# The last layer's expert results gated as they leave PSUM, and a final merge with all gathers issued at once

## The reference, cut to what matters

```python
hdn = jax.nn.silu(xb @ w1[e]) * (xb @ w3[e])      # per block of tokens of one expert
ys  = hdn @ w2[e]
y   = ys[dest] * flat_w[order][:, None]           # two rows a token, weighted
out = jax.ops.segment_sum(y, tok, num_segments=N)
xl  = xl + gt2 * out                              # gt2: one row of 1024, from the modulation vectors
return rmsnorm(xl, final_g)                       # after the last layer
```

## Time and profile before

| | us |
|---|---|
| median of 3 runs | 2804.71 (2804.48 to 2804.72) |
| the profiled execution's own time | 2803.35 |
| its span | 2801.6 |
| PE busy | 2571.0 (92% of the span) |
| DVE busy | 1082.8 (39%) |
| ACT busy | 865.5 (31%) |
| POOL busy | 478.1 (17%) |
| first weight chunk of layer 0's experts asked for | 984.9 |
| the same of layer 1 | 2173.9 |
| end of its last matmul | 2735.8 |

### The profile page before, as it was taken

How to read it: one execution, slowest core, us unless ns; L and a number is a source line. 1 busy time by engine, 2 the same in 40 slices (tenths; PEclk the granted TensorE clock), 3 DMA queues, 4 the chain that set the end, 5 groups by cost and what they waited for, 6 DMA issues and landing times. The chain is left out here.

```text
span 2801.6 us, 68712 instructions
## 1 busy us (share of the span) xinstructions
PE 2571.0 (92%) x28274; PEld 1803.8 (64%) x28275; DVE 1082.8 (39%) x2462; ACT 865.5 (31%) x1881; POOL 478.1 (17%) x590
## 2 busy tenths in 40 slices
PE   7999999999989849999999599999998699999990
PEld 6888788878745537777777484455444477777770
DVE  3134333433454532222222366556665322222225
ACT  3222322323210003333333355334500133333333
POOL 0111111121121012222222210000020122222223
PEclk9999999999999969999999799999999799999995
DMA  6322223132345287999999740000232999999995
GB/s 260 120 97 100 95 104 134 61 126 74 140 152 200 75 355 305 416 416 395 416 416 416 268 144 30 31 30 30 115 150 105 389 403 416 417 416 416 416 368 183
DMA packets 128670, 644.72 MB, mean 230 GB/s; under 512 B 18865, under 2 KB 31441, under 8 KB 72609
## 3 DMA queue, kind: packets, MB, share of 16 engines
q1 hardware_dynamic: 94912, 540.05, 48.5%
q0 software_dynamic: 17984, 57.16, 5.7%
q10 hardware_dynamic: 15648, 45.71, 4.2%
HBM read 578.29 MB, written 64.57 MB: 229 GB/s over the span
## 5 line engine op out<-in xcount | busy, mean ns | idle before, releaser
L1668 PE MATMUL PS<-wt,xT 128*32 128x256 f32 x13056 | 752.9, 381 | 38.3 <-DVE xT L1797 25.3
L1668 PEld LDWEIGHTS PS<-wt,xT 128*32 128x32 f32 x13056 | 513.0, 111 | 238.7 <-issue 47.9
L1613 ACT ACTIVATE y<-PS 32x256 f32<-32x256 f32 x816 | 306.3, 375 | 304.2 <-PE PS L1683 297.0
L1683 PE MATMUL PS<-wt,hidT 128*32 128x256 f32 x6528 | 395.2, 379 | 3.5 <-ACT y L1613 3.5
L1797 DVE STREAM_TRANSPOSE xT<-xg 128x256 f32<-128x256 f32 x206 | 91.8, 446 | 664.2 <-PE PS L1668 655.0
L1683 PEld LDWEIGHTS PS<-wt,hidT 128*32 128x32 f32 x6528 | 256.8, 110 | 99.3 <-issue 4.4
L720 PE MATMUL PS<-hT,slab 128*128 128x256 f32 x1280 | 296.2, 386 | 6.3 <-DVE low L613 3.5
L720 PEld LDWEIGHTS PS<-hT,slab 128*128 128x128 f32 x1280 | 239.9, 192 | 42.9 <-issue 6.5
L433 POOL TENSOR_SCALAR prob<-prob,inv 128x640 f32<-128x640 f32 (+2 forms) x80 | 130.3, 1629 | 662.2 <-DVE inv L628 662.2
L1573 POOL DMA_INDIRECT xg<-h_d,ib x212 | 208.3, 983 | 166.8 <-POOL ib L1570 166.0
L511 ACT ACTIVATE prob<-prob,low 128x640 f32<-128x640 f32 (+2 forms) x160 | 117.6, 735 | 300.2 <-DVE low L613 300.2
(11 more groups left out here) (247 smaller groups left out, 2653.4 us busy)
## 6 DMA issues: line engine op xcount, KB each, us to landing
wt<-in_w SPq DMA_DIRECT2D x256, 1024.0 KB, 11.9
wt<-in_w2s SPq DMA_DIRECT2D x128, 1024.0 KB
aw<-in_ada_w SPq DMA_DIRECT2D x48, 1024.0 KB, 4.9
ys_d<-y ACTq DMA_DIRECT2D x204, 128.0 KB
slab<-in_slabs SPq DMA_DIRECT2D x24, 512.0 KB, 3.3
tab<-in_tables SPq DMA_DIRECT2D x8, 1408.0 KB, 7.5
ys_d<-zero POOLq DMA_DIRECT2D x4, 2560.0 KB, 9.6
x_d<-x_p ACTq DMA_DIRECT2D x18, 512.0 KB, 4.8
```

The lines of the kernel that those rows point to most:

```text
L1613: ins = a.activation(y[rows, q * QD:q * QD + QD], PS[STRIP * q:STRIP * q + STRIP, DOWN, 0:QD], ACT.Copy)
L1668: mm = t.matmul(PS[32 * g:32 * g + 32, UP, 0:QD], xT[:, k * 32:k * 32 + 32], wt[b][:, q, c * 1024 + g * QD:c * 1024 + g * QD + QD], start= ...
L1683: mm = t.matmul(PS[32 * g:32 * g + 32, DOWN, 0:QD], hT_[:, k * 32:k * 32 + 32], wt[b][:, q, c * 1024 + g * QD:c * 1024 + g * QD + QD], sta ...
```

## The change

Five things are changed together.

- **Store in layer 1.** VectorE gets a new step in each turn of its loop, `gated`, behind `hidden`: it multiplies the whole PSUM tile (128x256) of the item before by a gate tile and writes it to a quarter of the columns of `y`. ScalarE no longer copies; its queue stores 128 partitions of 1 KB to the same 32 rows of `ys_d`. The first call, ahead of any result, only raises `y_ok`, and a last one behind the loop takes the last item.
- **Gate tile.** Four loads behind the first 12 weight chunks of layer 1 fill it (`early_loads`), and VectorE waits for them in `before_items_vector`.
- **Gathers.** All 16 are issued one after the other, each tile into its own buffers; nothing waits between them.
- **Merge.** As the rows are gated already, tiles 0, 2, 4, 6 and 7 take two VectorE operations for the sum, and tiles 1, 3 and 5 are summed by TensorE in PSUM, by products with the identity and with two diagonal matrices of the weights. ScalarE takes the squares and roots as before, VectorE the last product. Stores go straight from the tiles' buffers.
- **Recurrent vectors in layer 0.** The series moves behind the first transpose, into `behind_first_rows_vector`.

The core of the diff:

```diff
@@ class MergeMid
+            def behind_first_rows_vector(self, v):
+                r, n_ = self.lru, [7]
...
+                v.wait_ge(self.once, 7)
                 v.wait_ge(self.exp_ok, 1)
                 once(v.tensor_scalar(s2, z_, 2.0, None, ALU.add))
                 once(v.reciprocal(s2, s2))
...
@@ class MergeEnd
+            ON_PE = (1, 3, 5)
...
+                self.y = [(late1 if n < 6 else late2)(f"y_c1{n}", [P, 2, D]) for n in range(NTL)]
+                self.gate = flat(RLs[:, :, :])[:, 0:QD]
...
             def early_loads(self, sp):
-                pass
+                for q in range(4):
+                    at_q = mod_d[0, (NMOD + 5) * D + q * QD:]
+                    sp.dma_start(self.gate[32 * q:32 * q + 32, :], bass.AP(tensor=at_q.tensor, offset=at_q.offset, ap=[[0, 32], [1, QD]])
+                                 ).then_inc(self.gate_in, 16)
...
             def before_items_vector(self, v):
-                pass
+                v.wait_ge(self.gate_in, 64)
...
             def stores(self, sp):
                 for n in range(NTL):
                     sp.wait_ge(self.ob_ok, n + 1)
-                    sp.dma_start(out[0, n * P:(n + 1) * P, :], self.ob[n % 2][:, :]).then_inc(self.x_out[n % 2], 16)
...
+                    sp.dma_start(out[0, n * P:(n + 1) * P, :], self.y[n][:, 1, :]).then_inc(self.x_out, 16)
+                sp.wait_ge(self.x_out, 16 * NTL)
 
             def gather(self, g):
                 g.wait_ge(self.ys_ok, 1)
                 for n in range(NTL):
-                    if n >= 2:
-                        g.wait_ge(self.m_ok, n - 1)
-                    for k, yk in enumerate((self.y0, self.y1)):
-                        g.indirect_dma_start(out=yk[n % 2][:, :], out_offset=None, in_=ys_d[:, :],
+                    for k in range(2):
+                        g.indirect_dma_start(out=self.y[n][:, k, :], out_offset=None, in_=ys_d[:, :],
...
+            def tensor(self, t):
+                t.wait_ge(self.x_in, 16 * NTL)
+                for i, n in enumerate(self.ON_PE):
+                    t.wait_ge(self.dg_ok, 2 * i + 2)
+                    t.wait_ge(self.y_in[n], 32)
+                    for h in range(2):
+                        half = slice(h * 512, (h + 1) * 512)
+                        t.matmul(PS[:, 2 * i + h, :], ident[:, :], self.xa[:, n, half], start=True, stop=False)
+                        for k in range(2):
+                            mm = t.matmul(PS[:, 2 * i + h, :], self.diag[n][k][:, :], self.y[n][:, k, half], start=False, stop=(k == 1))
+                    mm.then_inc(self.pe_ok, 1)
...
                 def add(n):
...
+                    v.scalar_tensor_tensor(out=x, in0=x, scalar=tabs[1][:, 0, n:n + 1], in1=self.xa[:, n, :],
+                                           op0=ALU.mult, op1=ALU.add).then_inc(self.row_ok, 1)
+                    v.wait_ge(self.row_ok, 2 * m + 1)
+                    v.scalar_tensor_tensor(out=x, in0=self.y[n][:, 1, :], scalar=tabs[1][:, 1, n:n + 1], in1=x,
+                                           op0=ALU.mult, op1=ALU.add).then_inc(self.row_ok, 1)
...
                 add(0)
                 for n in range(NTL):
-                    if n + 1 < NTL:
+                    if n + 1 < NTL and n + 1 not in self.ON_PE:
                         add(n + 1)
                     norm(n)
@@ def experts
+            y_part = lambda j: y[:, j * QD:(j + 1) * QD]
...
+                    def store_gated(n, j):
+
+                        a.wait_ge(y_ok, n + 2)
+                        a.dma_start(ys_d[bass.ds(n * STRIP, STRIP), :].rearrange("t (q c) -> q t c", q=4), y_part(j)
+                                    ).then_inc(y_out[j], 16)
...
+                            if l:
+                                store_gated(n, j)
+                            else:
+                                store(n, i, j)
...
+                    def gated(n, i, j):
+
+                        v.wait_ge(used[5], n + 1)
+                        v.wait_ge(y_out[(j - 1) % DEEP], 16 * i + 16)
+                        v.tensor_tensor(y_part((j - 1) % DEEP), PS[:, DOWN, 0:QD], merge.gate, ALU.mult).then_inc(y_ok, 1)
+
                     rows_T(0, 0, 0)
+                    merge.behind_first_rows_vector(v)
                     with v.Fori(0, count) as i:
...
                             hidden(n)
+                            if l:
+                                gated(n, i, j)
+                    if l:
+                        gated(count * DEEP, count, 0)
```

More of the change, by code:

```diff
@@ L1357, in begin @@
                 nm = lambda x: sem(f"{x}_c1")
[L1358 to L1362, removed]
+                self.gate_in, self.fin_in, self.x_in, self.x_out = nm("gate"), nm("fin"), nm("x_in"), nm("x_out")
+                self.y_in = [gather_sem(f"y_in{n}_c1") for n in range(NTL)]
+                self.dg_ok, self.pe_ok, self.row_ok, self.sum_ok, self.sqrt_ok, self.rs_ok, self.ob_ok = (
+                    nm(x) for x in ("diag", "on_pe", "rows_made", "sum", "sqrt", "rs", "ob"))
             def early_loads(self, sp):
-                pass
+                for q in range(4):
+                    at_q = mod_d[0, (NMOD + 5) * D + q * QD:]
+                    sp.dma_start(self.gate[32 * q:32 * q + 32, :], bass.AP(tensor=at_q.tensor, offset=at_q.offset, ap=[[0, 32], [1, QD]])
+                                 ).then_inc(self.gate_in, 16)
             def early_scalar(self, a):
@@ L1427, in scalar @@
[L1427 to L1432 removed]
+                for n in self.ON_PE:
+                    for k in range(2):
+                        a.activation(self.diag[n][k][:, :], ident[:, :], ACT.Identity, scale=tabs[1][:, k, n:n + 1]).then_inc(self.dg_ok, 1)
+                a.activation(self.rt[:, NTL:NTL + 1], epst[:, :], ACT.Sqrt)
@@ L1596, in _ @@
                     count = a.value_load(npi[0:1, 0:1], **most)
-                    a.sem_inc(y_ok, 1)
+                    if not l:
+                        a.sem_inc(y_ok, 1)
                     for j in range(DEEP):
-                        a.sem_inc(y_out[j], 16)
+                        a.sem_inc(y_out[j], 32 if l and j == DEEP - 1 else 16)
                     def tanh(n):
@@ L1622, in _ @@
                             tanh(n + 1)
-                            store(n, i, j)
+                            if l:
+                                store_gated(n, j)
+                            else:
+                                store(n, i, j)
                     for j in range(DEEP):
-                        a.wait_ge(y_out[j], 16 * count + 16)
+                        a.wait_ge(y_out[j], 16 * count + (32 if l and j == DEEP - 1 else 16))
                     a.sem_inc(ys_ok, 1)
```

82 lines of the change are left out of this document (35 added, 47 removed).

## The result

The changed kernel takes 2921.71 us (median of 4 runs, 2920.53 to 2924.3), the kernel before 2804.72 beside it (2804.48 to 2806.67): the ratio is 1.042 (95% interval 1.0408 to 1.0433). I had forecast 2882 and a range to 2918; the direction held, and the time is 3.7 us outside the range.

The account below looks back on a forecast made before the run. TensorE, busy 92% of the span, was taken to bound the kernel. Terms -5.4 + 100.3 - 0.2 - 17.1 = +77.6 us on the 2801.6 us span gave 2879.2, a forecast time of 2882.3 us, range 2840 to 2918.

Parts of the forecast that it names:

- Four engines: Layer 1's gated store, outer dimension 4: runs on four DMA engines, the same each time, 1.29 us more an item each.
- The loop: Layer 1's item loop: the four engines' added store load makes the last weights late, +100.3 us.
- What would show it: Signs in the profile after: TensorE waits for weights, items of 6.2 us, mean DMA share about 0.85, twelve engines idle.
- Start of layer 1: Gate loads queued behind twelve weight chunks delay the first transpose 2 to 6 us, covered while weights set the pace: 0.
- Start of layer 0: The series for the decay rates moves behind the first transpose, which then starts earlier: -5.4 us.
- To the first gather: From the last down product to the first final gather: shorter until the store's issue, longer store, together -0.2 us.
- The merge: First final gather to the end: transfers set the pace, pairs 3.23 us apart, stores delay the last pair: -17.1 us.
- low-clock price: Final merge: an instruction of TensorE's tiles estimated at 0.9 us at half clock, against 0.45 us at full clock.
- low-clock rival: Final merge: TensorE's low clock sets its pace, -7.8 us instead of -17.1, 2892 us with four engines; chance 0.07.
- the rival of 16 engines: Layer 1's stores use all 16 engines or wander over them, so the kernel gains: 2784.7 us; chance 0.20.

Follow-up runs that it names:

- the last kernel: The changed kernel with the store in four transfers, the gate's loads in front of the weights, and VectorE's merge sums two tiles ahead: 2774.12 us, ratio 0.99.

## Why the prediction was wrong in size, point by point

- **Four engines** (right). The short packets said so before, and 132 packets a store say so after. That they are the same four each time fits as well: the weights are left on four engines' worth of share, and the stores take turns with just those.
- **The loop, +100.3 against +138.7** (this term failed). The step was "four engines get 1.29 us more an item. Every weight chunk is spread over all 16 and is there only when the slowest has finished": I priced the store by the engine time of its pieces and made the weights wait for it. In the changed kernel it is the store that waits for the weights. Its 32 packets an engine take turns with 8 KB packets, 11 us a store in place of 1.63; four buffers and the queue cover some items, then ScalarE stands in the issue and TensorE behind it. The weights catch up, twelve engines run idle and then all weights are through, the stores go at 1.5 us each, and it begins again. 25 of the loop's stores took 4 us or more to issue; 25 items at 10.8 us instead of 5.18 would be 140 us more, an estimate that covers the loss. The mechanism that I had priced exists: the four engines do fall behind, and with 2 KB packets, where the turns are short, it costs 60 us. In the change as made TensorE never waited for it, and what it would cost at 8 KB without the turns was not measured. So the term came as near as it did by luck, for a reason that was not the acting one.
- **What would show it** followed the same error. TensorE waiting for weights: not one such wait, and 26 only with 2 KB packets. A mean share near 0.85: 0.81 from 2210 to 2700, as a mean of stretches near 1.0 and others at 0.2 to 0.3. Twelve engines do idle in the latter, but just there TensorE runs at its old pace, so it is no sign of a wait for DMA. An item at 6.2 us: 6.7.
- **The rule of the Trainium skill** ("DMA: Bandwidth & Descriptors", section "Why a DMA increments its semaphore by 16 and not by 1") was right: an outer 4 gives four engines. I had not weighed another section of that page, "Queues, rings and completion order", by which an engine goes round its queues packet by packet. The trace agrees that turns go by count and not by bytes (beside 8 KB neighbours a store of 1 KB pieces took 10.6 to 11.2 us and one of 512 B pieces 10.3), and it shows one piece of each queue in a turn (78 to 73).
- **Start of layer 1, covered: 0 against +7.0** (wrong). The size was near (2 to 6 us forecast), the cover was not there: I let the weights set the pace behind it, and they never did. 6.6 us came back when the gate was loaded first. It was my own condition "with all 16 engines it is on the path", which in fact held for four as well.
- **Start of layer 0, -5.4 against -3.0.** Right for the part by itself (-6.3, -3.6 to -9.0); this kernel's load landed 2.3 us later.
- **To the first gather, -0.2** (right: -0.1).
- **The merge, -17.1 against -21.6.** The pairs came at the pace I gave them: in the last kernel tile 0's rows are used at 2738.60 and tile 4's at 2750.90, 3.08 us a pair against 3.23. Wrong was that each output store delays the last pair by 1.25 us. The rows were all there, and VectorE ran with gaps of at most 0.15 us from 2901.57 on:

```profile
2901.57 0.16 DVE L1469 RECIPROCAL rs_c<-rt_c 128x1 f32<-128x1 f32 x1 [3.56 <-ACT rt_c L1436]
...
2913.80 1.28 DVE L1460 SCALAR_TENSOR_TENSOR y_c<-y_c,w,xa_c 128x1024 f32<-128x1024 f32 x1
...
2918.14 1.28 DVE L1471 SCALAR_TENSOR_TENSOR y_c<-y_c,rs_c,fin_c 128x1024 f32<-128x1024 f32 x1
```

  Tile 7's first sum starts 31.0 us behind the first gather and not 35.3: that is 4.3 of the 4.5 us. TensorE's tiles were done by the times I gave (squares start 17.3, 22.4 and 27.6 us behind the first gather, against 18, 23 and 32), the last 4.4 us sooner. My low-clock price of 0.9 us an instruction was not what its source gives: 0.45 x 6.24 / 3.66 is 0.77. Only the low-clock rival hung on it, and it didn't occur.

All that is not the loop's store was a gain: -17.7 us by the table at the top, and with the store on 16 engines 2781.98 us, 22 under the kernel before, as the rival of 16 engines had it (2784.7).

## What to carry to other kernels

A transfer's outer dimension decided here how many DMA engines it used, and 4 is a trap when the partitions fall into quarters: four transfers of 32 rows cost ScalarE's queue 1.2 us more an item and saved 140 us. Price a small transfer beside a full weight stream by its packets per engine times the neighbour's packet plus its own (here 32 x 0.36 us, some 6% too much), compare that with the time between two of them, and ask what stands behind the engine that issues it. A row loaded for all partitions behind a queue of megabyte loads landed with the last of them; put it in front.

## What the runs showed of the hardware that was not expected

- Issuing a store took ScalarE 0.55 us, and up to 7.5 us once stores before it hadn't drained; the engine does nothing else meanwhile, though nothing in its program waits.
- On an engine that had both to move, one 1 KB piece of the store and one 8 KB weight packet went in turn: 73 and 78 in 6 us on four engines, where the store alone got 527 packets through in 6 us.
- Weights in 2 KB packets ran at 389 GB/s at a full DMA share, against 416 in 8 KB packets; TensorE waited for them even with the store on 16 engines.
- 128 pieces of 512 B took 0.028 us each and those of 1 KB 0.047: neither price says how long the transfer lasts beside other traffic.
